# Softmax numerators of three attentions normalised by GpSimd, and a new order of TensorE's work in each block

## The chip, the cores and the metric

One NeuronCore of a Trainium2 (trn2) chip. The metric is the device time of one execution in microseconds (us), the median over runs.

## The reference, cut to what matters

Two transformer layers' worth of blocks over 1024 tokens of width 1024. Three of the stages are attentions with 8 heads of 64 columns: one with a band mask whose entries are log-counts ("attn1"), and two without a mask, in which 8 query heads share 2 key/value heads and the result is multiplied by a gate ("attn2_0", "attn2_1"). Per head, in float32:

```python
scores = q @ k.T * scale            # attn1: + log(count) inside the bands, -1e30 outside
p = softmax(scores, axis=-1)
o = p @ v                           # attn2: o * gate
```

Everything else (feed-forward layers, projections, an mLSTM, a Fourier stage, norms) is outside the change.

## The kernel before, in words

Each engine has its own program, and they meet only through semaphores (`x.at(name, u)` is the value to wait for; `.mark` the signal that is given). All attentions run the same code. The work is cut into blocks u = 0..63 (n = 64), one for 128 queries of one head, and w = u//2 counts pairs of blocks.

TensorE (`attention` of the tensor program, lines 839 to 907), at its step u: `scores(u)` (L858, four 512-column matmuls into one of two PSUM pairs), `turn_over(u-1)` (L868, eight 128x128 transposes of the numerators into the single PSUM pair `p_t`, half 0 then half 1), and the product with V: at odd u the row sums of the two blocks are spread over all partitions (`spread_sum`, L879, a matmul of ones with a diagonal of reciprocals) and then `times_v(w, 0)` with w=(u-3)//2 (L891, eight 256-column matmuls with the high parts); at even u `times_v(w, 1)` with the low parts. `times_v(w, 0)` waits for the low parts of block 2w+1.

ScalarE (lines 1262 to 1309), step u: `half_result` at odd u (copies the lower 64 rows of the V product, L1269; at the end of two heads also the high part of the heads, L1274), `num_high(u-1)` (L1283, the two halves of `p_t` rounded into `th`), `numerators(u)` (L1292, exp with the row sum as accumulator), `diagonal(u-1)` (L1299, identity times the reciprocal).

VectorE (lines 1812 to 1867), step u: `maximum(u)` (attn1: L1824 adds the mask and takes the maximum, L1827 negates it; attn2: L1829), `results` at odd u (L1843 adds the halves of the product, L1847 multiplies by the spread reciprocals; at the end of two heads the gate L1853 and the low part of the heads L1856), `low_parts(u-1)` (L1835, the two halves of `p_t` minus the high parts), the reciprocal of row sum u-1 (L1867).

GpSimd (lines 2130 to 2174) issues the loads of q, k, v, gates, the mask of attn1 (L2227) and, once the last scores are done, the loads of the other half of the mixer's output (`load_mix`, L2174). It computes nothing. SyncE's queue (lines 2234 to 2316) streams the weights through two raw buffers and issues the mLSTM's loads and its last store (L2285).

The order of the work is the order in which each engine's `for u` loop is written; every engine executes its own instructions strictly in that order. After an attention `out_proj` (L600) starts with the k tiles in the order of a list; for attn2 it is tiles 0, 1, 2 of the attention's own heads, then the loaded ones, then tile 3.

Of the kernel before, what the change touches and what calls it, by code (L numbers as in the profile page):

```python
# [13 lines left out]
P = 128  # L14
S = 1024
# [269 lines left out]
def memory(nc, ctx):  # L285
# [105 lines left out]
    def attention_tiles(name, scope, between=None):  # L391
# [10 lines left out]
        a.nu = rings(f"{name}_num", 2, [P, S], F32, scope)  # L402
        a.th = rings(f"{name}_th", 2, [P, ST, 256], F32R, scope)
        a.tl = rings(f"{name}_tl", 2, [P, ST, 256], F32R, scope)
        a.sm = rings(f"{name}_sm", 2, [P, 4], F32, scope)
        a.dg = [t.sqh[1][:, (i + 1) * P:(i + 2) * P] for i in range(3)]
        a.ones = t.sqh[1][:, 0:P]
        a.tm = [t.sqh[0][0:64, i * 256:(i + 1) * 256] for i in range(2)]
# [9 lines left out]
    with ExitStack() as ma:  # L418
        m.mixa = split("mix1a", [P, 4, S], ma)
        with ExitStack() as sc:  # L420
            m.at = attention_tiles("attn1", sc)
            m.at.mask = sb("attn1_mask", [P, 1920], F32, sc)
        mix_tiles(m, "mix1", ma)
# [51 lines left out]
def program_of(nc, ctx, ins, out):  # L475
# [22 lines left out]
    scored, num_turned, spread, pv_done = (signal(n, "PE") for n in ("scored", "num_turned", "spread", "pv_done"))  # L498
# [5 lines left out]
    diag, half_res, mix_hi = (signal(n, "ACT") for n in ("diag", "half_res", "mix_hi"))  # L504
# [6 lines left out]
    mix_lo, ml_dve, conv_dve, four_dve = (signal(n, "DVE") for n in ("mix_lo", "ml_dve", "conv_dve", "four_dve"))  # L511

# [11 lines left out]
    at_const, at_gate, mo_in = signal("at_const_in", "POOL", 16), signal("at_gate_in", "POOL", 16), loaded("mo_in", "POOL", 2)  # L524
# [36 lines left out]
    for n, (kind, _, _, _) in enumerate(plan):  # L561
        if kind == "w":
            split_no[n] = len(split_at)
            split_at.append(n)

# [12 lines left out]
    def tensor_program(e):  # L578
# [260 lines left out]
        def attention(name, mix, kv_of, a, masked):  # L839
# [5 lines left out]
            p_o = ps.take(e, (name, "o"), res_done, name, n // 2 - 1)  # L845
# [16 lines left out]
            def turn_over(u):  # L862
                e.wait_ge(*exped.at(name, u))
                for h in range(2):
                    if u >= 1:
                        e.wait_ge(*num_lo.at(name, u - 1, h))
                    for j in range(4):
                        mm = e.transpose(p_t.half[h][:, j * P:(j + 1) * P], a.nu[u % 2][:, (4 * h + j) * P:(4 * h + j + 1) * P],  # L868
# [3 lines left out]
            def spread_sum(u):  # L872
                w = u // 2
                e.wait_ge(*diag.at(name, u))
                if u == 0:
                    e.wait_ge(*at_const.at(name))
                if w >= 2:
                    e.wait_ge(*res_done.at(name, w - 2))
                mm = e.matmul(p_o.half[w % 2][:, 256 + (u % 2) * P:256 + (u % 2 + 1) * P], a.ones, a.dg[u % 3],  # L879
                              start=True, stop=True)  # L880
                mm.then_inc(*spread.mark(name, u))

            def times_v(w, part):
                hd, i = (2 * w) // ST, (2 * w) % ST
                kv = kv_of(hd)
# [1597 lines left out]
```

## Time and profile before

| | us |
|---|---|
| median of 3 runs (lowest, highest) | 3885.12 (3881.82, 3887.04) |
| the profiled execution | 3889.09 |
| its span in the profile | 3887.3 |
| TensorE busy / VectorE / ScalarE / GpSimd | 3536.8 / 1918.4 / 1351.0 / 149.0 |
| mean granted TensorE clock, share of full speed | 0.951 |

Busy times are sums over the whole span. A row of a timeline says start, duration, engine, line, operation, output<-inputs, shape and count; "x8" with a duration is a merged group, from the first one's start to the last one's end, and the square bracket says how long the engine had been idle and what ended that. A matmul's record is longer than the step to the next one, since they overlap; the distance between starts is the cost.

### The profile page before, as it was taken

Reading aid. Unit: us, or ns where it says so; the run is one execution under the profiler, and the core shown is the slowest. Engines: PE = TensorE matmul, PEld = TensorE weight load, DVE = VectorE, ACT = ScalarE, POOL = GpSimd, SP = SyncE. Lnnn points to the kernel's source line nnn. Section 1 sums busy time; section 2 is a strip of 40 time slices with the busy share of each in tenths; the row PEclk is TensorE's granted clock in tenths of the full one; section 3 lists DMA queues with packets and bytes.
Section 4 is the critical chain, followed back from the end, with each engine's and each line's share of the span. In section 5 each row is a group of like instructions: output and inputs, shape, how many; then the busy total and the mean of one; then the engine's idle time right before and its main releaser. Section 6 shows DMA issues by size and latency. Waiting matters only on the chain.

```text
span 3887.3 us, 41660 instructions
## 1 busy us (share of the span) xinstructions
PE 3536.8 (91%) x17310; PEld 2888.9 (74%) x17310; DVE 1918.4 (49%) x2459; ACT 1351.0 (35%) x1874; POOL 149.0 (4%) x261
## 2 busy tenths in 40 slices
PE   5999999988987698899999998889898988998987
PEld 3888888866975587778888885678887745887875
DVE  6233333366427698353333335622588365137964
ACT  4111111154222388221111113521487064126843
POOL 0000000000100110000000000010100001000000
PEclk8999999999996799999999999999999989999998
DMA  5222221213741453122222221231611103243111
GB/s 194 89 83 71 82 92 66 76 66 98 184 168 39 82 87 61 44 87 71 90 72 78 76 76 38 77 111 60 180 28 33 49 23 102 85 131 98 28 39 44
DMA packets 146619, 316.58 MB, mean 81 GB/s; under 512 B 32616, under 2 KB 96908, under 8 KB 135936
## 3 DMA queue, kind: packets, MB, share of 16 engines
q1 hardware_dynamic: 84880, 216.80, 16.1%
q0 software_dynamic: 61552, 97.12, 10.5%
q8 instruction: 138, 2.26, 0.2%
q14 instruction: 49, 0.40, 0.0%
HBM read 261.79 MB, written 52.09 MB: 81 GB/s over the span
## 4 chain that ended last, share of the span: by engine, by line
PE 79%; DVE 11%; ACT 5%; issue 3%; DMA 1%; POOL 0%; SPq 0%; ACTq 0%; DVEq 0%; POOLq 0%
PE psum L600 56%; PE psum L868 4%; PE psum L891 4%; PE psum L858 4%; PE psum L1015 2%; PE psum L627 2%; PE psum L944 1%; PE psum L698 1%; PE psum L879 1%; DVE h_lo L1495 1%; PE psum L934 1%; ACT attn_th L1283 1%; ACT attn_num L1292 1%; PE psum L792 1%; DVE p_u L1582 0%
## 5 line engine op out<-in xcount | busy, mean ns | idle before, releaser
L600 PE MATMUL psum<-h_hi,w_hi 128*128 128x512 f32 x2112 | 835.0, 395 | 45.0 <-DVE h_lo L1495 26.8
L600 PE MATMUL psum<-h_lo,w_hi 128*128 128x512 f32 x2112 | 826.6, 391 | 0.0
L600 PE MATMUL psum<-h_hi,w_lo 128*128 128x512 f32 x2112 | 826.2, 391 | 0.0
L600 PEld LDWEIGHTS psum<-h_hi,w_hi 128*128 128x128 f32 x2112 | 399.1, 189 | 142.7 <-issue 46.1
L600 PEld LDWEIGHTS psum<-h_lo,w_hi 128*128 128x128 f32 x2112 | 399.4, 189 | 83.1 <-issue 2.9
L600 PEld LDWEIGHTS psum<-h_hi,w_lo 128*128 128x128 f32 x2112 | 399.1, 189 | 83.5
L1051 ACT ACTIVATE w_hi<-w_raw 128x2048 fp32r<-128x2048 f32 (+2 forms) x147 | 249.1, 1695 | 572.1 <-PE psum L600 468.1
L1445 DVE TENSOR_TENSOR w_lo<-w_raw,w_hi 128x2048 fp32r<-128x2048 f32 (+2 forms) x147 | 296.9, 2020 | 262.2 <-ACT w_hi L1051 261.5
L1544 DVE TENSOR_TENSOR gate<-gate,psum 128x1024 f32<-128x1024 f32 x44 | 53.7, 1221 | 608.2 <-PE psum L600 608.2
L600 PE MATMUL psum<-a_hi,w_hi 128*128 128x512 f32 x704 | 274.3, 390 | 3.4 <-DVE a_lo L1546 3.4
L600 PE MATMUL psum<-a_hi,w_lo 128*128 128x512 f32 x704 | 274.1, 389 | 0.0
L600 PE MATMUL psum<-a_lo,w_hi 128*128 128x512 f32 x704 | 274.1, 389 | 0.0
L868 PE MATMUL psum<-mats,attn_num 128*128 128x128 f32 x1536 | 211.7, 282 | 58.1 <-ACT attn_num L1292 56.9
L868 PEld LDWEIGHTS psum<-mats,attn_num 128*128 128x128 f32 x1536 | 177.0, 144 | 112.8 <-ACT attn_num L1292 100.4
L1835 DVE TENSOR_TENSOR attn_tl<-psum,attn_th 128x512 fp32r<-128x512 f32 x384 | 246.4, 681 | 16.3 <-ACT attn_th L1283 15.3
L1560 DVE SCALAR_TENSOR_TENSOR x<-psum,cols,x 128x1024 f32<-128x1024 f32 x80 | 102.7, 1284 | 261.9 <-PE psum L600 261.9
L1283 ACT ACTIVATE attn_th<-psum 128x512 fp32r<-128x512 f32 x384 | 209.1, 594 | 23.6 <-PE psum L868 18.4
L1116 ACT ACTIVATE a_hi<-gate 128x1024 fp32r<-128x1024 f32 x44 | 46.7, 1061 | 478.8 <-DVE gate L1544 478.8
L1829 DVE TENSOR_REDUCE attn_sm<-psum 128x1 f32<-128x1024 f32 x128 | 156.4, 1223 | 39.2 <-PE psum L858 24.8
L858 PE MATMUL psum<-attn_kh,attn_q 128*128 128x512 f32 x384 | 156.0, 406 | 3.9 <-DVE fo_u L1978 2.2
L1111 ACT ACTIVATE gate<-psum 128x1024 f32<-128x1024 f32 x44 | 45.3, 1029 | 318.5 <-PE psum L600 318.5
L858 PE MATMUL psum<-attn_kl,attn_q 128*128 128x512 f32 x384 | 155.7, 406 | 0.0
(332 smaller groups left out, 5703.5 us busy)
## 6 DMA issues: line engine op xcount, KB each, us to landing
w_raw<-in_w_ada SPq DMA_DIRECT2D x52, 1024.0 KB, 5.0
w_raw<-in_w_gu SPq DMA_DIRECT2D x44, 1024.0 KB, 5.4
w_raw<-in_w_in SPq DMA_DIRECT2D x34, 1024.0 KB, 4.8
w_raw<-in_dft SPq DMA_DIRECT2D x16, 1024.0 KB, 5.2
w_raw<-in_w_down SPq DMA_DIRECT2D x24, 512.0 KB, 3.6
w_raw<-in_w_out SPq DMA_DIRECT2D x12, 1024.0 KB, 5.2
w_raw<-in_w_down SPq DMA_DIRECT2D x16, 640.0 KB, 4.3
qk_hi_scratch<-p_out_hi POOLq DMA_DIRECT2D x18, 512.0 KB, 2.9
```

The lines of the kernel that those rows point to most:

```text
L600: mm = e.matmul(p.half[h], a[:, k * width + m * P:k * width + (m + 1) * P], b(k)[:, h * HALF:(h + 1) * HALF], start=(k == order[0] and i = ...
L627: mm = e.matmul(p.full[:, j * 256:(j + 1) * 256], b[:, k, (tt0 + j) * P:(tt0 + j + 1) * P], a[:, k * 256:(k + 1) * 256], start=(k == 0 and ...
L858: mm = e.matmul(p_s[u % 2].half[h], a.q[hd % 2][:, i * P:(i + 1) * P], k_[kv % 2][:, h * HALF:(h + 1) * HALF], start=(j == 0), stop=(j == 1))
L868: mm = e.transpose(p_t.half[h][:, j * P:(j + 1) * P], a.nu[u % 2][:, (4 * h + j) * P:(4 * h + j + 1) * P], ident)
L891: mm = e.matmul(p_o.half[w % 2][:, 0:256], a.v[kv % 2][:, j, :], (a.th, a.tl)[part][w % 2][:, j, :], start=(part == 0 and j == 0), stop=(p ...
L1015: mm = e.matmul(p.half[g][:, 0:256], b[:, g, k, tb * P:(tb + 1) * P], a[:, k * 256:(k + 1) * 256], start=(tb == 0 and k == 0 and i == 0), ...
L1051: e.activation(halves_of(n)[0], raw_of(n), ACT.Identity).then_inc(*w_hi.mark(n))
L1283: e.activation(a.th[w % 2][:, 4 * h:4 * h + 4, c], ps.of[(name, "t")].half[h].rearrange("p (j q) -> p j q", j=4), ACT.Identity).then_inc(* ...
L1445: e.tensor_tensor(lo, raw_of(n), hi.bitcast(F32), ALU.subtract).then_inc(*w_done.mark(n))
L1560: e.scalar_tensor_tensor(out=t.x[:, dd, :], in0=ps.of[("down", n, i, dd)].full, scalar=cols[:, 8 + dd:9 + dd], in1=t.x[:, dd, :], op0=ALU. ...
L1829: e.tensor_reduce(m[:, 1:2], p.full, AX.X, ALU.max, negate=True).then_inc(*maxed.mark(name, u))
L1835: e.tensor_tensor(a.tl[w % 2][:, 4 * h:4 * h + 4, c], ps.of[(name, "t")].half[h].rearrange("p (j q) -> p j q", j=4), a.th[w % 2][:, 4 * h: ...
```

## The change

Six things are changed. (1) GpSimd multiplies each block's numerators in SBUF by the reciprocal of their row sum (`num_scaled`), and TensorE transposes block u only after that; `spread_sum`, `diagonal` and VectorE's multiplication by the spread reciprocals go. (2) TensorE's step u is now scores(u), the V product, turn_over(u-2); the parts of the V product alternate, high parts at even u, low parts at odd u. ScalarE's and VectorE's `num_high` and `low_parts` follow one block later. (3) Results are taken over four blocks (z = 64x512 instead of 64x256), at every fourth step, after the exp of that step on ScalarE and after the low parts on VectorE. (4) The gate's product in attn2 goes from VectorE to GpSimd; the high and low parts of the heads are made at u=22+16pp and u=23+16pp. (5) In attn1 the maximum is taken as a minimum of negated scores, so the negation L1827 goes. (6) The mask is loaded by SyncE's queue into a raw weight buffer, the gates by SyncE's queue too; numerators and sums have three buffers; the keys are loaded in smaller portions, released by scores, not by V products. The load of ones goes.

```diff
-        a.nu = rings(f"{name}_num", 2, [P, S], F32, scope)
+        a.nu = rings(f"{name}_num", 3, [P, S], F32, scope)
-        a.sm = rings(f"{name}_sm", 2, [P, 4], F32, scope)
+        a.sm = rings(f"{name}_sm", 3, [P, 4], F32, scope)
+    t.mix1.at.mask = t.raw[first_out1 % RAW][:, 0:1920]
...
             def turn_over(u):
-                e.wait_ge(*exped.at(name, u))
+                e.wait_ge(*num_scaled.at(name, u))
...
-            def spread_sum(u):
...
             def times_v(w, part):
+                kv, z = kv_of(hd), w // 2
                 if part == 0:
                     e.wait_ge(*num_lo.at(name, 2 * w + 1, 1))
+                    if w % 2 == 0 and z >= 2:
+                        e.wait_ge(*res_done.at(name, z - 2))
...
                 if u < n:
                     scores(u)
-                if 1 <= u <= n:
-                    turn_over(u - 1)
-                if u >= 3 and u % 2 == 1 and u < n + 3:
-                    spread_sum(u - 3)
-                    spread_sum(u - 2)
-                    times_v((u - 3) // 2, 0)
-                if u >= 4 and u % 2 == 0:
-                    times_v((u - 4) // 2, 1)
+                if u >= 4:
+                    times_v((u - 4) // 2, u % 2)
+                if 2 <= u < n + 2:
+                    turn_over(u - 2)
...
+            def half_result(z):
+                e.wait_ge(*pv_done.at(name, 2 * z + 1))
+                if z >= 2:
+                    e.wait_ge(*res_done.at(name, z - 2))
+                e.activation(a.tm[z % 2], ps.of[(name, "o")].half[z % 2][64:128, :], ACT.Identity).then_inc(*half_res.mark(name, z))
+            def heads_high(pp):
+                e.wait_ge(*(res_done.at(name, 4 * pp + 3) if masked else og_gated.at(name, pp)))
+                e.activation(mixa[0][:, pp, :], a.og[:], ACT.Identity).then_inc(*mix_hi.mark(mix, "a", pp))
...
+            for u in range(n + 8):
+                if 2 <= u < n + 2:
+                    num_high(u - 2)
                 if u < n:
                     numerators(u)
-                if 1 <= u <= n:
-                    diagonal(u - 1)
+                if u >= 8 and u % 4 == 0 and u < n + 8:
+                    half_result((u - 8) // 4)
+                if u >= 22 and (u - 22) % 16 == 0:
+                    heads_high((u - 22) // 16)
...
-                    e.wait_ge(*maxed.now())
-                    e.tensor_scalar(m[:, 1:2], m[:, 0:1], -1.0, None, ALU.mult).then_inc(*maxed.mark(name, u))
...
+            def results(z):
+                hh, pp = (z // 2) % 2, z // 4
+                e.wait_ge(*half_res.at(name, z))
+                if z % 4 == 0 and pp:
+                    e.wait_ge(*mix_lo.at(mix, "a", pp - 1))
+                e.tensor_tensor(a.og[64 * hh:64 * hh + 64, (z % 2) * HALF:(z % 2 + 1) * HALF], ps.of[(name, "o")].half[z % 2][0:64, :],
+                                a.tm[z % 2], ALU.add).then_inc(*res_done.mark(name, z))
...
+            for u in range(n + 8):
                 if u < n:
                     maximum(u)
+                if 1 <= u < n + 1:
+                    s = a.sm[(u - 1) % 3]
                     e.wait_ge(*exped.at(name, u - 1))
+                    e.reciprocal(s[:, 3:4], s[:, 2:3]).then_inc(*recip.mark(name, u - 1))
+                if 2 <= u < n + 2:
+                    low_parts(u - 2)
+                if u >= 8 and u % 4 == 0 and u < n + 8:
+                    results((u - 8) // 4)
+                if u >= 23 and (u - 23) % 16 == 0:
+                    heads_low((u - 23) // 16)
...
+        def attention(name, a, n_kv, gated):
             n = A_HEADS * ST
-            e.dma_start(a.ones, ins["mats"][MAT["ones"]]).then_inc(*at_const.mark(name))
             load_kv(name, a, 1)
+            for u in range(n + 8):
+                hd, i = u // ST, u % ST
+                if u < n:
+                    s, m = a.nu[u % 3], a.sm[u % 3]
+                    e.wait_ge(*recip.at(name, u))
+                    e.tensor_scalar(s[:], s[:], m[:, 3:4], None, ALU.mult).then_inc(*num_scaled.mark(name, u))
+                if i == 7 and hd + 2 < A_HEADS:
+                    load_q(name, a, hd + 2)
+                if i in (0, 1) and 1 <= hd < n_kv - 1:
+                    load_k(name, a, hd + 1, i)
+                if i == 3 and 1 <= hd < n_kv - 1:
+                    load_v(name, a, hd + 1)
+                if gated and u >= 20 and (u - 20) % 16 == 0:
+                    pp = (u - 20) // 16
+                    e.wait_ge(*res_done.at(name, 4 * pp + 3))
+                    e.wait_ge(*at_gate.at(name, pp))
+                    e.tensor_tensor(a.og[:], a.og[:], a.g[:], ALU.mult).then_inc(*og_gated.mark(name, pp))
...
+        weights(first_out1 + RAW)
         mlstm()
+        e.wait_ge(*w_done.at(first_out1))
+        e.dma_start(t.mix1.at.mask[:], ins["band"]).then_inc(*at_const.mark("attn1"))
+        e.wait_ge(*maxed.at("attn1", A_HEADS * ST - 1))
         for l in range(2):
             weights(first_block(("dft", l, 0, 0)) + 1 + RAW)
             fourier(l)
+            weights(first_block(("out2", l, 0)) + RAW)
+            attention_gates(l)
```

## Rows read from the trace of the kernel before

**Rows 1.** The page's first part: busy us (share of the span) and instructions

```profile
PE 3536.8 (91%) x17310; PEld 2888.9 (74%) x17310; DVE 1918.4 (49%) x2459; ACT 1351.0 (35%) x1874; POOL 149.0 (4%) x261
```

**Rows 2.** Windows of attn1 and attn2_1: length; busy PE, PEld, DVE, ACT, POOL; clock; DMA

```profile
1316.00:1544.00 228.00, 206.09 (x1417) 179.14 (x1417) 197.16 (x452) 183.38 (x356) 29.59 (x52) 0.95 0.49 81
...
3525.00:3742.00 217.00, 199.08 (x1387) 176.14 (x1388) 190.05 (x323) 178.30 (x355) 13.56 (x25) 0.96 0.17 40
```

**Rows 3.** Timeline of attn2_0, TensorE over one pair of blocks

```profile
2841.36 1.09 PE L868 MATMUL psum<-mats,attn_num 128*128 128x128 f32 x8
...
2842.29 0.61 PE L879 MATMUL psum<-sq 128*128 128x128 f32 x4
...
2842.66 1.19 PE L891 MATMUL psum<-attn_th,attn_v 128*128 128x256 f32 x8
...
2843.69 0.40 PE L858 MATMUL psum<-attn_kh,attn_q 128*128 128x512 f32 x1
...
2844.61 1.04 PE L868 MATMUL psum<-mats,attn_num 128*128 128x128 f32 x8
...
2845.41 1.20 PE L891 MATMUL psum<-attn_tl,attn_v 128*128 128x256 f32 x8
...
2847.48 1.09 PE L868 MATMUL psum<-mats,attn_num 128*128 128x128 f32 x8
```

**Rows 4.** The same timeline, ScalarE and VectorE beside it

```profile
2842.06 1.08 ACT L1283 ACTIVATE attn_th<-psum 128x512 fp32r<-128x512 f32 x2
...
2843.03 1.12 ACT L1292 ACTIVATE attn_num<-psum,attn_sm 128x1024 f32<-128x1024 f32 x1
...
2843.49 1.29 DVE L1835 TENSOR_TENSOR attn_tl<-psum,attn_th 128x512 fp32r<-128x512 f32 x2
```

**Rows 5.** Timeline near the start of attn2_0, where neither engine has a queue

```profile
2798.52 1.09 PE L868 MATMUL psum<-mats,attn_num 128*128 128x128 f32 x8 [0.91 <-ACT attn_num L1292]
2799.21 1.09 ACT L1283 ACTIVATE attn_th<-psum 128x512 fp32r<-128x512 f32 x2 [0.46 <-PE psum L868]
...
2799.84 1.29 DVE L1835 TENSOR_TENSOR attn_tl<-psum,attn_th 128x512 fp32r<-128x512 f32 x2 [0.45 <-ACT attn_th L1283]
```

**Rows 6.** Timeline, one pass of VectorE over 128x1024 from SBUF to SBUF, eight times

```profile
3757.64 4.90 DVE L1988 TENSOR_SCALAR x<-x 128x1024 f32<-128x1024 f32 x8
```

**Rows 7.** Timeline, the start of attn1

```profile
1322.90 0.58 POOL L2227 DMA_DIRECT2D attn_mask<-in_band  x1 [10.71 <-DMA mix_scratch<-ml_o]
...
1328.53 1.23 DVE L1824 CUSTOM_DVE_ANT_0 attn_num<-psum,attn_mask 128x1024 f32<-128x1024 f32 x1 [12.29 <-DMA sq<-in_mats]
...
1331.36 1.97 PE L868 MATMUL psum<-mats,attn_num 128*128 128x128 f32 x8 [10.96 <-ACT attn_num L1292]
```

**Rows 8.** First out_proj matmul behind attn1; first transposes, first out_proj and loaded tile of attn2_1

```profile
1541.52 0.40 PE L600 MATMUL psum<-mix1a_hi,w_hi 128*128 128x512 f32 x1
...
3529.93 1.98 PE psum L868 x8
...
3743.66 0.40 PE L600 MATMUL psum<-mix2a_hi,w_hi 128*128 128x512 f32 x1
...
3751.36 0.80 PE L600 MATMUL psum<-mix21b_hi,w_hi 128*128 128x512 f32 x1 [5.48 <-DVE mix21b_lo L1872]
```

**Rows 9.** The page's DMA part: count, KB each, median us from issue to landing

```profile
mix_t<-mix_scratch POOLq DMA_DIRECT2D x12, 512.0 KB, 4.2
```

**Rows 10.** Timeline of attn1: TensorE behind the second and the third interruption, to the second-next scores

```profile
1445.44 1.09 PE L868 MATMUL psum<-mats,attn_num 128*128 128x128 f32 x8 [2.14 <-ACT attn_num L1292]
...
1450.73 0.40 PE L858 MATMUL psum<-attn_kh,attn_q 128*128 128x512 f32 x1
...
1497.50 1.09 PE L868 MATMUL psum<-mats,attn_num 128*128 128x128 f32 x8 [2.15 <-ACT attn_num L1292]
...
1499.86 0.63 PE L858 MATMUL psum<-attn_kh,attn_q 128*128 128x512 f32 x1
...
1504.14 0.40 PE L858 MATMUL psum<-attn_kh,attn_q 128*128 128x512 f32 x1
```

More of the change, by code:

```diff
@@ L511, in program_of @@
     mix_lo, ml_dve, conv_dve, four_dve = (signal(n, "DVE") for n in ("mix_lo", "ml_dve", "conv_dve", "four_dve"))
+    num_scaled, og_gated = (signal(n, "Pool") for n in ("num_scaled", "og_gated"))
     const_in, x_in = signal("const_in", "SP", 16), loaded("x_in", "SP", 2)
@@ L564, in program_of @@
             split_at.append(n)
+    first_out1 = next(n for n, entry in enumerate(plan) if entry[3] == ("out1", 0))
+    t.mix1.at.mask = t.raw[first_out1 % RAW][:, 0:1920]
     def place_before(n):
@@ L889, in times_v @@
                         e.wait_ge(*v_in[kv % 2].at(name, kv))
+                    if w % 2 == 0 and z >= 2:
+                        e.wait_ge(*res_done.at(name, z - 2))
                 for j in range(ST):
-                    mm = e.matmul(p_o.half[w % 2][:, 0:256], a.v[kv % 2][:, j, :], (a.th, a.tl)[part][w % 2][:, j, :],
-                                  start=(part == 0 and j == 0), stop=(part == 1 and j == ST - 1))
+                    mm = e.matmul(p_o.half[z % 2][:, (w % 2) * 256:(w % 2 + 1) * 256], a.v[kv % 2][:, j, :],
+                                  (a.th, a.tl)[part][w % 2][:, j, :], start=(part == 0 and j == 0),
+                                  stop=(part == 1 and j == ST - 1))
                 if part == 1:
@@ L2214, in block2 @@
             e.wait_ge(*fo_stored.at(l))
[L2215 removed]
+            attention(at_name, m.at, 2, True)
             load_mix(m, mix, at_name, 4)
@@ L2223, in gpsimd_program @@
         fence("attn1")
-        for h in (1, 2):
-            e.wait_ge(*st_stored[h % 2].at("ml", h))
-        e.wait_ge(*ml_stored3.at())
-        e.dma_start(t.mix1.at.mask[:], ins["band"]).then_inc(*at_const.mark("attn1", "mask"))
-        attention("attn1", t.mix1.at, A_HEADS, None)
+        ml_drained(e)
+        attention("attn1", t.mix1.at, A_HEADS, False)
         load_mix(t.mix1, "mix1", "attn1", 0)
@@ L2289, in fourier @@
             e.wait_ge(*passed("PE", f"fourier{l}"))
-            for j in range(2):
+            for j in (0, 1):
                 e.wait_ge(*st_stored[j % 4].at(f"p2b{l}", j))
@@ L2387, in shape_constants @@
     count = (j <= 64).astype(int) + ((j % 4 == 0) & (j <= 256)) + (j % 16 == 0)
-    band = np.where(count > 0, np.log(np.maximum(count, 1)), NEG).astype(f)
+    band = np.where(count > 0, -np.log(np.maximum(count, 1)), -NEG).astype(f)
     sel = np.zeros((36, 8, P), f)
```

145 lines of the change are left out of this document (48 added, 97 removed).

## The prediction

> **What bounds the kernel now.** I read the page first, then the windows of the three attentions, then their timelines. The page says that TensorE is the engine of the whole kernel [rows 1]; the change touches only the attentions, so what counts is what ends last there. The windows show three engines nearly full: in attn1's 228 us TensorE has 206, VectorE 197, ScalarE 183; in attn2_1's 217 us 199, 190 and 178 [rows 2]. Nobody has slack of more than 20%, so an order that makes one engine wait for another costs at once. The timeline gives the beat: two blocks take 6.12 us in attn2 (2841.36 to 2847.48 [rows 3]). TensorE issues in a pair: transposes 2 x 0.80 (2844.61 to 2845.41), V products 2 x 1.04 (2842.66 to 2843.69), scores 2 x 0.92 (2843.69 to 2844.61), the spreading 0.37 (2842.29 to 2842.66, all [rows 3]), and the rest is a short wait for the exp. GpSimd is nearly idle.
>
> The stage lengths, first transposes to first out_proj matmul: attn1 1331.36 to 1541.52 = 210.2 [rows 7, 8], attn2_1 3529.93 to 3743.66 = 213.7 [rows 8]. Attn2_0 has the same pattern and is taken as equal. In them are four interruptions per attention, at each end of two heads, in which TensorE waits for 2 us and more, as 2.14 [rows 10].
>
> **The change, part by part.** *Removed from TensorE:* 0.37 of spreading per pair. If TensorE were alone, a pair would take 2 x (0.92 + 1.04 + 0.80) = 5.52. *Removed elsewhere:* ScalarE loses its diagonals, VectorE the multiplications behind the results and in attn1 the negation. That shortens two engines that already fit beside TensorE, so I count it at nothing; the order below leaves them waiting anyway.
>
> *The new order* is the term that decides. At an even step u, TensorE issues scores(u) and then the V product of the pair whose second block, u-3, was transposed at the very end of step u-1. Before, a whole further step lay between. What this needs is shown where nobody has a queue [rows 5]: transposes start 2798.52, ScalarE's high parts 2799.21, VectorE's low parts 2799.84 to 2801.13, that is 2.61 us, 0.1 less when the transposes themselves had no wait, and 0.05 for the signal: 2.6. TensorE fills only 0.80 + 0.92 = 1.72 of it. So it waits 0.9 in every pair, and its first matmul behind a wait costs 0.1 more (transposes behind a wait take 0.93 to the next group, 2841.36 to 2842.29, against 0.80 [rows 3]). Base pair: 2.60 + 0.10 + 1.04 (V, high) + 0.80 (transposes) + 0.92 (scores) + 1.04 (V, low) = 6.50.
>
> *Results every fourth step.* Count from an odd step's transposes, time 0. Even step: V at 2.6, transposes 3.64, high parts at 4.28, exp at 5.26 (step 0.98 for two halves [rows 4]), which ends at 6.54 with its accumulator; only then half_result, now 64x512, taken as 0.6 like one half of L1283: 7.14. VectorE was done with the low parts at 6.1 and waits; its result runs 7.17 to 7.77 (0.6, like one half of L1835). Behind it are queued the next maximum (1.22, the L1824 row [rows 7]) and reciprocal (0.1): 9.09. Only then low_parts of the odd step: 10.37, while TensorE, which transposed at 6.40, would have had it at 9.0. It waits 1.42 longer, each fourth step, 14 times per attention (steps 8 to 60).
>
> *GpSimd's pass* (128x1024, SBUF to SBUF, scalar per partition) is in no row. Nearest: VectorE's same form takes 4.90/8 = 0.61 [rows 6], ScalarE's and VectorE's passes at full width 1.12 [rows 4] and 1.23 [rows 7]. I bound it by 0.6 below and twice the slowest, 2.5, above, and take 1.2, an engine's ordinary pass. It has room: the reciprocal of block 0 comes at 8.99, and its transposes are due at 11.46, so up to 2.2 it is hidden under the waits above; GpSimd's DMA issues (0.58 [rows 7], at most two behind one pass) fit beside it too. The gate's product there: 1.2 likewise, same ends.
>
> *Ends of heads* (three inside each attention): heads_high (1.06) on ScalarE delays the next high parts by about 0.5, heads_low on VectorE the next maximum by less than its slack: 0.8 each, 2.4 in all. The old interruptions go, since they are in the old lengths.
>
> New length: 31.5 pairs x 6.50 = 204.8, + 14 x 1.42 = 19.9, + last V products 2.6 + 0.1 + 2.08 = 4.8, + 2.4, + 1 for the slow clock at the start = 232.9. Attn1 +22.7; each attn2 +19.2.
>
> *Start.* Attn1's mask now goes behind SyncE's store, which is why GpSimd waited until 1322.90, and needs no buffer of the mLSTM. VectorE still waits for that store, so its first maximum is at about 1323.0, not 1328.53 [rows 7]: -5.5. From first maximum to first transposes 2.83 before, now maximum and exp 2.5, reciprocal and signals 0.3, GpSimd's pass 1.2: 4.0, so +1.2. Net -4.3. Attn2, where TensorE waited for the exp alone: +1.4 each for the reciprocal and the pass. *Tail.* In attn2 load_mix is now queued behind GpSimd's last gate product, which waits for the last result; before it left at the last scores. From TensorE's end: half 0.8, result 1.6, gate 2.9, landing 4.2 after that [rows 9], high part and low part 2.3: 9.5, against 7.7 before (3743.66 to 3751.36 [rows 8]): +1.8 each. In attn1 it is issued behind the last scaling and still covered. The weight block that the mask keeps out is issued at the last maximum, more than 20 us ahead of its use: 0. Gates and keys on other queues: 0, each has over five steps of cover; without it a load of some 4 us would show per head.
>
> Sum: attn1 22.7 - 4.3 = 18.4; attn2 2 x (19.2 + 1.4 + 1.8) = 44.8; together +63. The profiled execution took 3889.09, 4 above the median; the sum is a difference inside it and I put it on the median: 3885.1 + 63 = **3948**.
>
> The page "GPSIMD Engine Reference" of the Trainium skill (section Elementwise — side-by-side cycle accounting) speaks against using that engine: about 2.6 cycles per element for two inputs, 1.03 where the loop is port-bound. By the first rate, an estimate from that page is 2.4 us per pass, over the 2.2 of cover, about 0.2 x 48 = +10 and 3958; by the second it is 1.04 and the sum stands. No row here can tell.
>
> **The rivals.**
> (a) *TensorE is the bound and the new order is harmless:* the place is the V product's wait. If the low parts came back inside 1.72 us of the transposes' start, pairs would take 5.6 and the lengths 187: -23 and -27 twice, with start and tail: 3885 - 75 = 3810. It decides when the mean pair falls below 6.46. For it: TensorE really loses work. Against it: [rows 5], and the order in the code.
> (b) *No stall from the results* (ScalarE's half_result finds a gap): -14 x 1.42 x 3 = -60: 3888. Against: an engine works in order.
> (c) *The clock falls.* Waits of 2.14 us in attn1 left the clock at the 2.4 GHz level in one case, but in the next TensorE went on at 1.2 GHz: a score matmul of 0.63 instead of 0.40 at 1499.86 [rows 10], and from the transposes to the second-next scores it took 1497.50 to 1504.14 = 6.64 instead of 1445.44 to 1450.73 = 5.29 [rows 10], 1.35 more. The new kernel has 14 waits of 2.3 in each attention: all 42 x 1.35 = +57, 4005; a third of them 3967.
> (d) *GpSimd is slower than its cover:* at 3.0 us its pass holds the transposes of even steps 0.8 and 0.5 in four blocks: 1.3 x 48 = +62, 4010.
>
> **How the numbers follow.** Forecast (3920 to 3975) 0.48, (a) 0.12, (b) 0.13, (c) 0.15, (d) 0.12. The range takes in (b), (c) and (d) and leaves (a) out: 3885 to 4012. A measurement can tell about 0.2%, 7.8 us. (b) lies on the border: 0.06 within it, 0.02 faster, 0.05 slower. So faster 0.14, same 0.06, slower 0.80.
>
> **What would show it.** Score starts in the timeline: 14.4 us per four blocks and TensorE waiting for L1835's successor before the V product, 0.9 and 2.3 in turn; VectorE idle before the result until ScalarE's half. TensorE waiting for GpSimd instead is (d); an even beat of 2.8 per block is (a); score matmuls of 0.63 in mid-attention are (c). The forecast is wrong if pairs stay under 6.4 or if the waits are put down to something other than the low parts.

## The result and the profile after

| | us |
|---|---|
| kernel before, median of 4 runs (lowest, highest) | 3883.55 (3881.82, 3887.04) |
| changed kernel, median of 4 runs (lowest, highest) | 4020.82 (4017.36, 4024.97) |
| ratio with its 95% interval | 1.0353 [1.0335, 1.0371] |
| span of the profiled execution, before / after | 3887.3 / 4015.5 |

The change makes the kernel 3.5% slower, 137 us. I had forecast +63 and a range up to 4012; the direction was right, the size too small, and the result lies 9 us above the range.

The page of the changed kernel: the engines' busy time, the shares of the chain that ended last, and five groups (busy us, mean ns of one | idle time before them, and what ended it).

```profile
PE 3548.8 (88%) x16926; PEld 2876.7 (72%) x16926; DVE 1861.8 (46%) x2243; ACT 1279.0 (32%) x1634; POOL 706.9 (18%) x449
...
PE 68%; DVE 13%; POOL 7%; ACT 7%; issue 3%; DMA 2%; SPq 0%; ACTq 0%; DVEq 0%; POOLq 0%
...
L2154 POOL TENSOR_SCALAR attn_num<-attn_num,attn_sm 128x1024 f32<-128x1024 f32 x192 | 545.6, 2846 | 161.6 <-DVE attn_sm L1845 160.7
...
L871 PE MATMUL psum<-mats,attn_num 128*128 128x128 f32 x1536 | 228.6, 296 | 47.9 <-POOL attn_num L2154 45.8
...
L885 PE MATMUL psum<-attn_th,attn_v 128*128 128x256 f32 x768 | 120.9, 302 | 104.6 <-DVE attn_tl L1822 104.6
```

Against [rows 1] every engine but GpSimd issues less: TensorE 384 matmuls fewer, VectorE 216 instructions, ScalarE 240. TensorE is nevertheless busy for 12 us longer: more of its matmuls run at the lower clock (below), and those behind a wait have longer records. GpSimd goes from 4% to 18%, and stands in the chain that ended last with 7%. Its pass takes 2.846 us. TensorE's idle time of the attentions sits mainly at two places: 104.6 us before the first V product, put down to VectorE's low parts, and 45.8 us before the transposes, put down to GpSimd.

Windows of attn1 and attn2_1 (length; busy PE, PEld, DVE, ACT, POOL; clock; DMA), which answer to [rows 2]:

```profile
1324.00:1582.00 258.00, 202.93 (x1270) 170.53 (x1271) 174.47 (x338) 155.12 (x274) 208.26 (x110) 0.95 0.31 63
3635.00:3867.00 232.00, 185.23 (x1152) 157.13 (x1151) 155.11 (x245) 138.10 (x246) 174.24 (x72) 0.94 0.10 26
```

In attn1 no engine is full any more: GpSimd 81%, TensorE 79%, VectorE 68%. Before, TensorE had 90% and VectorE 86% [rows 2]. The stages are bound by latency now (each engine waits in turn for the result of another), and longer. Their starts and ends in the timeline, which answer to [rows 7, 8]:

```profile
1329.45 1.97 PE L871 MATMUL psum<-mats,attn_num 128*128 128x128 f32 x8 [2.43 <-POOL attn_num L2154]
...
1582.28 0.40 PE L603 MATMUL psum<-mix1a_hi,w_hi 128*128 128x512 f32 x1
...
3608.29 1.11 ACT L1285 ACTIVATE attn_num<-psum,attn_sm 128x1024 f32<-128x1024 f32 x1
...
3612.70 1.97 PE L871 MATMUL psum<-mats,attn_num 128*128 128x128 f32 x8 [1.08 <-POOL attn_num L2154]
...
3867.04 0.63 PE L603 MATMUL psum<-mix2a_hi,w_hi 128*128 128x512 f32 x1
...
3877.47 0.79 PE L603 MATMUL psum<-mix21b_hi,w_hi 128*128 128x512 f32 x1 [6.98 <-DVE mix21b_lo L1856]
```

Attn1 from its first transposes to the first out_proj matmul: 1582.28 - 1329.45 = 252.8, before 210.2; attn2_1: 3867.04 - 3612.70 = 254.3, before 213.7. Attn2_0 has 253.9 (2833.53 to 3087.47), before 213.7 (2791.66 to 3005.37), as the forecast had assumed. The three differences, 42.6 + 40.2 + 40.6 = 123.4, are nearly all of the 128.2 by which the spans of the two profiled executions differ.

One stretch of attn1, all engines. It shows both waits and the queue behind them:

```profile
1402.27 0.59 ACT L1260 ACTIVATE sq<-psum 64x512 f32<-64x512 f32 x1
...
1402.89 0.68 DVE L1831 TENSOR_TENSOR attn_o<-psum,sq 64x512 f32<-64x512 f32 x1 [0.94 <-ACT sq L1260]
1403.18 1.09 ACT L1273 ACTIVATE attn_th<-psum 128x512 fp32r<-128x512 f32 x2 [0.32 <-PE psum L871]
...
1403.61 1.23 DVE L1812 CUSTOM_DVE_ANT_0 attn_num<-psum,w_raw 128x1024 f32<-128x1024 f32 x1
...
1404.83 1.27 DVE L1822 TENSOR_TENSOR attn_tl<-psum,attn_th 128x512 fp32r<-128x512 f32 x2
...
1405.03 5.67 POOL L2154 TENSOR_SCALAR attn_num<-attn_num,attn_sm 128x1024 f32<-128x1024 f32 x2 [1.71 <-DVE attn_sm L1845]
...
1406.16 1.23 PE L885 MATMUL psum<-attn_th,attn_v 128*128 128x256 f32 x8 [1.64 <-DVE attn_tl L1822]
...
1407.92 1.09 PE L871 MATMUL psum<-mats,attn_num 128*128 128x128 f32 x8 [0.54 <-POOL attn_num L2154]
```

Read it from the top. ScalarE makes the half result after its exp (1402.27), VectorE waited 0.94 for it and adds (1402.89). Behind that, in VectorE's own order, stands the next maximum (1403.61), and only then the low parts (1404.83). ScalarE's high parts had been there since 1404.27. TensorE, waiting for the low parts, has its V product at 1406.16 after 1.64 us of nothing. That is the forecast's results stall, with its links in the order drawn; the idle time is shorter than the 2.3 drawn. The last two rows are what I had priced at zero: GpSimd's pass started at 1405.03, ends at 1407.88, and the transposes follow it by 0.04.

A stretch in which the clock had fallen, in attn2_0, is the other thing to see:

```profile
2910.38 1.87 PE L871 MATMUL psum<-mats,attn_num 128*128 128x128 f32 x8 [0.55 <-POOL attn_num L2154]
2911.90 0.78 PE L861 MATMUL psum<-attn_kh,attn_q 128*128 128x512 f32 x1
2912.48 0.63 PE L861 MATMUL psum<-attn_kl,attn_q 128*128 128x512 f32 x1
```

The score matmuls last 0.63, where they last 0.40 at the 2.4 GHz level [rows 3]; the granted clock from 2910.38 to 2913 is 0.53. Before the fall TensorE had waited 1.61 and then 0.55. Counted over the three attentions, 90 of the 768 score matmuls last 0.55 us or more, 33 of 768 in the kernel before. Windows of attn2_0 (length; busy PE, PEld, DVE, ACT, POOL; clock; DMA), first the kernel before, then the changed one:

```profile
2791.66:3005.37 213.71, 201.22 (x1400) 178.30 (x1401) 188.28 (x322) 175.72 (x352) 10.09 (x20) 0.97 0.17 38
```

```profile
2833.53:3087.47 253.94, 206.87 (x1268) 175.54 (x1269) 170.94 (x271) 151.64 (x270) 192.14 (x78) 0.93 0.12 25
```

### The profile page after: what moved, and what is told of

Its sections match the earlier page's. It is cut to its first block, busy times and chain, and to the rows that moved or that the text cites. A ratio compares the mean times of both kernels' runs of the same rounds, so it can differ in the third digit from the quotient of the medians.

```text
span 4015.5 us, 40194 instructions
## 1 busy us (share of the span) xinstructions
PE 3548.8 (88%) x16926; PEld 2876.7 (72%) x16926; DVE 1861.8 (46%) x2243; ACT 1279.0 (32%) x1634; POOL 706.9 (18%) x449
## 4 chain that ended last, share of the span: by engine, by line
PE 68%; DVE 13%; POOL 7%; ACT 7%; issue 3%; DMA 2%; SPq 0%; ACTq 0%; DVEq 0%; POOLq 0%
PE psum L603 54%; POOL attn_num L2154 6%; PE psum L1006 2%; PE psum L871 2%; PE psum L630 2%; DVE attn_tl L1822 2%; ACT attn_th L1273 1%; DVE attn_sm L1816 1%; PE psum L885 1%; PE psum L935 1%; PE psum L701 1%; DVE h_lo L1482 1%; PE psum L925 1%; ACT attn_num L1285 1%; PE psum L861 1%
## 5 line engine op out<-in xcount | busy, mean ns | idle before, releaser
L2154 POOL TENSOR_SCALAR attn_num<-attn_num,attn_sm 128x1024 f32<-128x1024 f32 x192 | 545.6, 2846 | 161.6 <-DVE attn_sm L1845 160.7
L871 PE MATMUL psum<-mats,attn_num 128*128 128x128 f32 x1536 | 228.6, 296 | 47.9 <-POOL attn_num L2154 45.8
L885 PE MATMUL psum<-attn_th,attn_v 128*128 128x256 f32 x768 | 120.9, 302 | 104.6 <-DVE attn_tl L1822 104.6
L885 PEld LDWEIGHTS psum<-attn_th,attn_v 128*128 128x128 f32 x768 | 100.5, 195 | 145.1 <-DVE attn_tl L1822 145.1
L861 PE MATMUL psum<-attn_kh,attn_q 128*128 128x512 f32 x384 | 180.1, 469 | 22.4 <-ACT attn_num L1285 12.6
```

What stands on the lines that cost most here:

```text
L861: mm = e.matmul(p_s[u % 2].half[h], a.q[hd % 2][:, i * P:(i + 1) * P], k_[kv % 2][:, h * HALF:(h + 1) * HALF], start=(j == 0), stop=(j == 1))
L885: mm = e.matmul(p_o.half[z % 2][:, (w % 2) * 256:(w % 2 + 1) * 256], a.v[kv % 2][:, j, :], (a.th, a.tl)[part][w % 2][:, j, :], start=(part ...
L2154: e.tensor_scalar(s[:], s[:], m[:, 3:4], None, ALU.mult).then_inc(*num_scaled.mark(name, u))
```

## The experiments

All are edits of the changed kernel unless said otherwise. Where no interval is given it is one time, beside one or more runs of the kernel before on the same chip; those runs lie up to 11 us apart (3878.72 to 3890.14), so differences of some 10 us between such times are weak.

### How long GpSimd's pass is, and what the order costs without it

```diff
-                    e.tensor_scalar(s[:], s[:], m[:, 3:4], None, ALU.mult)
+                    e.tensor_scalar(s[:, 0:8], s[:, 0:8], m[:, 3:4], None, ALU.mult)
```

> GpSimd multiplies only 8 of the 1024 columns of each block, so that its pass costs almost nothing and every wait and the order stay; the other columns stay unscaled. Theory A (two causes: my forecast's waits of the order, and on top of them a GpSimd pass of 2.85 us where I had 1.2): what is left is my forecast without the pass in start and tail, about 3943 us. Rival B (the GpSimd pass alone is the cause, the new order costs nothing): TensorE-bound pairs, about 3810 us. Rival C (a pass of GpSimd is not what holds the transposes, its semaphores or the clock are): stays near 4020.

**Measured: 3946.39**, the kernel before 3885.36 beside it, so +61.0. TensorE's idle groups:

```profile
L871 PE MATMUL psum<-mats,attn_num 128*128 128x128 f32 x1536 | 210.8, 283 | 0.4
...
L885 PE MATMUL psum<-attn_th,attn_v 128*128 128x256 f32 x768 | 118.1, 297 | 123.5 <-DVE attn_tl L1822 123.5
```

The wait for GpSimd is gone from the transposes (0.4 us), the wait before the V product stays and even grows. So 61 of the 137 us are there without the pass, and about 75 come from its length. The 61 belong to the new order with all else that was changed beside it; the edits of order below show that the order is what costs. A stretch of attn2_1, without the end of a head and at the full clock:

```profile
3605.23 0.48 PE L861 MATMUL psum<-attn_kh,attn_q 128*128 128x512 f32 x1
...
3608.27 1.22 PE L885 MATMUL psum<-attn_th,attn_v 128*128 128x256 f32 x8 [1.87 <-DVE attn_tl L1822]
...
3610.12 0.48 PE L861 MATMUL psum<-attn_kh,attn_q 128*128 128x512 f32 x1
...
3614.69 1.22 PE L885 MATMUL psum<-attn_th,attn_v 128*128 128x256 f32 x8 [0.64 <-DVE attn_tl L1822]
...
3619.29 0.48 PE L861 MATMUL psum<-attn_kh,attn_q 128*128 128x512 f32 x1
```

The waits of 1.87 and 0.64 come in turn. Four blocks take 3619.29 - 3605.23 = 14.06 by the score starts; I had forecast 14.4. That is the shortest that occurs: over the 42 groups of four blocks with a result in them the mean is 14.67, since the ends of heads and stretches at the lower clock come on top.

With half the columns (`s[:, 0:512]` in the same line; the others stay unscaled here too):

> GpSimd multiplies 512 of 1024 columns, so that its pass is about 1.45 us, near the 1.2 of the forecast; the other columns stay unscaled. Theory A: below the 2.2 us of cover, so about 3948 us, no more than 6 above the run with 8 columns. Rival B: a pass of 1.45 fits beside TensorE too: about 3815 us. Rival C: near 4020.

**Measured: 3960.63.** The pass takes 1.563 us. And the full product, written with another instruction:

```diff
-                    e.tensor_scalar(s[:], s[:], m[:, 3:4], None, ALU.mult)
+                    e.tensor_tensor(s[:], s[:], m[:, 3:4].to_broadcast([P, S]), ALU.mult)
```

> Full pass, but as a tensor_tensor product with the reciprocal column broadcast along the row, since the gate's product of that form took 2.36 us and the tensor_scalar pass 2.85. Theory A: a pass of 2.4 is 0.2 over the cover of 2.2 on every other block, about 3960 to 3985 us, much under 4020. If the pass takes 2.85 us in this form too, about 4020.

**Measured: 3956.34**, with the whole computation done. The four GpSimd groups, of the kernels with 8 columns, 512 columns, the other instruction, and (last row) the deeper kernel with the first instruction:

```profile
L2154 POOL TENSOR_SCALAR attn_num<-attn_num,attn_sm 128x8 f32<-128x8 f32 x192 | 58.6, 305 | 573.0 <-DVE attn_sm L1845 573.0
```

```profile
L2154 POOL TENSOR_SCALAR attn_num<-attn_num,attn_sm 128x512 f32<-128x512 f32 x192 | 300.1, 1563 | 341.0 <-DVE attn_sm L1845 340.8
```

```profile
L2154 POOL TENSOR_TENSOR attn_num<-attn_num,attn_sm 128x1024 f32<-128x1024 f32 x192 | 363.4, 1893 | 282.1 <-DVE attn_sm L1845 281.9
```

```profile
L2155 POOL TENSOR_SCALAR attn_num<-attn_num,attn_sm 128x1024 f32<-128x1024 f32 x192 | 546.0, 2859 | 7.3 <-DVE attn_sm L1846 5.8
```

So passes of 0.31, 1.56, 1.89 and 2.85 us give 3946, 3961, 3956 and 4021; the three stage lengths together are 697.5, 702.8, 705.3 and 761.1. From 0.3 up to 1.9 the pass costs 10 to 14 us in all, hardly more than two runs of one kernel can differ, of which the three starts of the attentions, where it has no cover, are 3 x 1.6 = 5; from 1.9 to 2.85 it costs 64 more. There is a cover, and its end lies between those two values, where the forecast had put it (2.2).

### V product and transposes in the other order

```diff
-                if u >= 4:
-                    times_v((u - 4) // 2, u % 2)
                 if 2 <= u < n + 2:
                     turn_over(u - 2)
+                if u >= 4:
+                    times_v((u - 4) // 2, u % 2)
```

> Full GpSimd pass, but TensorE transposes before the V product in each step, the rest as changed. The V product then no longer waits for the low parts, but the scaled numerators are due 1.04 us earlier. Theory A with the chain scores 1.13, maximum 1.23, reciprocal 0.25, pass 2.85 between the scores of step u-1 and the transposes of step u: a block of about 4.5 us instead of 4.04, so slower than the changed kernel, about 4100 us. Rival (the V product's wait is the larger cost): faster than 4020, about 3960.

**Measured: 4050.13**, 29 us slower than the changed kernel: the sign that my theory named, at well under half the size. The waits of attn2_0, 2870 to 3060 (total us, times, longest):

```profile
ACT attn_th L1273 <- PE psum L871: 74.0, 44, 3.0
...
PE psum L871 <- POOL attn_num L2154: 45.4, 30, 2.7
```

The low parts no longer hold TensorE: the wait before the V product has been bought off with a longer one before the transposes. The chain is scores, maximum, exp, reciprocal, pass, transposes, and with transposes first it has lost the V product's 1.04 as cover. With a pass of this length either order stalls. What the order is worth can only be seen with the pass out of the way, so the next two use 8 columns.

### Results at the head of the step, then the order, with a short pass

```diff
             for u in range(n + 8):
+                if u >= 8 and u % 4 == 0 and u < n + 8:
+                    half_result((u - 8) // 4)
                 if 2 <= u < n + 2:
...
                     numerators(u)
-                if u >= 8 and u % 4 == 0 and u < n + 8:
-                    half_result((u - 8) // 4)
...
-                if 2 <= u < n + 2:
-                    low_parts(u - 2)
                 if u >= 8 and u % 4 == 0 and u < n + 8:
                     results((u - 8) // 4)
+                if 2 <= u < n + 2:
+                    low_parts(u - 2)
```

> Again GpSimd multiplies only 8 of the 1024 columns (the rest stays unscaled), TensorE's order as changed, but ScalarE takes half_result at the head of its step, before the high parts and the exp, and VectorE takes results before its low parts. Theory A: the longer wait of each fourth step goes, 14 x 1.42 x 3 = 60 us off the 3946 of the run with 8 columns: about 3886 us, and the wait of about 0.9 before the V product stays in every pair. Rival (the two waits are one and the same, or results are not what delays the low parts): within 15 us of 3946.

**Measured: 3870.76**, 75.6 below the same kernel without this edit, or 72.5 when each is taken against the kernel before on its own chip (forecast of the stall's price: 60). A pair now is the same nearly everywhere; only at the ends of heads is it up to 0.4 longer:

```profile
2869.23 0.48 PE L861 MATMUL psum<-attn_kh,attn_q 128*128 128x512 f32 x1
...
2871.05 1.22 PE L885 MATMUL psum<-attn_th,attn_v 128*128 128x256 f32 x8 [0.64 <-DVE attn_tl L1822]
...
2872.90 0.48 PE L861 MATMUL psum<-attn_kh,attn_q 128*128 128x512 f32 x1
...
2875.65 0.48 PE L861 MATMUL psum<-attn_kh,attn_q 128*128 128x512 f32 x1
```

2875.65 - 2869.23 = 6.42, made of 3.67 and 2.75, against a forecast base pair of 6.50. The 0.64 (idle time; the start is 1.05 after the last score matmul's) is the wait that the order of the code makes. Attn2_0 and the sums over the three stages, first without the early results, then with them:

```profile
2809.03:3042.32 233.29, 191.96 (x1269) 168.81 (x1268) 170.97 (x271) 151.13 (x270) 32.48 (x78) 0.96 0.13 29
...
sum 697.52, PE 573.69 PEld 504.63 DVE 513.25 ACT 455.87 POOL 109.91; mean PE 191.23 PEld 168.21 DVE 171.08 ACT 151.96 POOL 36.64
```

```profile
2781.17:2988.68 207.51, 183.92 (x1269) 161.80 (x1268) 169.48 (x271) 149.06 (x270) 32.61 (x78) 0.99 0.15 32
...
sum 622.86, PE 551.93 PEld 485.51 DVE 509.33 ACT 449.60 POOL 110.27; mean PE 183.98 PEld 161.84 DVE 169.78 ACT 149.87 POOL 36.76
```

The stages are 74.7 us shorter. TensorE, which issues the same matmuls in the same order, is idle for 52.9 us less and busy for 21.8 less, and its granted clock goes from 0.96 to 0.99. So the stall itself cost some 53 us, 42 x 1.22 = 51 by the score starts (four blocks in 14.06, now in 2 x 6.42), and the rest goes with the clock that had fallen behind the waits. Then the transposes come first as well:

> As the run before it (8 columns scaled, early results), and TensorE transposes before the V product. Theory A: no wait is left but TensorE's own work, 2.76 us a block, lengths of about 183 us: about 3800 us. Rival (VectorE with 2.65 us a block and ScalarE keep TensorE from it): about 3850 us.

**Measured: 3802.97**, another 67.8 off. A window of its attn2_0:

```profile
2790.00:2840.00 50.00, 48.91 (x351) 43.70 (x350) 46.70 (x76) 41.55 (x76) 9.73 (x23) 1.00 0.13 33
```

TensorE is busy for 98% of it at a clock of 1.00, and most blocks take 2.76, which is half of the 5.52 I had worked out for TensorE alone; with one longer block in four the mean is 2.88. Behind the first 12 us of each stage no score matmul lasts 0.55 us or more. The kernel is 79 us faster than the one before. That takes together the spreading matmuls, the waits for the exp and the old interruptions at the ends of heads (see the last experiment); no run here separates them. The same early results with the full product, V first and the faster instruction:

> Complete: the changed kernel with two edits, GpSimd's pass as tensor_tensor (1.9 us) and the early half_result and results; TensorE's order stays V first. Theory A: a pass of 1.9 us stays under the cover, and the pair is 6.4 us with the short wait before the V product alone: 3871 (the run with 8 columns) and up to 10 for the pass in start, tail and the blocks where a DMA issue stands behind it: 3871 to 3885 us, so about the kernel before. Rival: the pass and the results add up, near 3956.

**Measured: 3884.07** beside 3883.74: as fast as the kernel before, within the noise. Removing the results stall and a third of the pass pays back the whole loss, and no more; V still waits (22 us of idle time in each stage).

### A complete kernel with one block more between the steps

It has the faster instruction, transposes before V, both a block later, four buffers for the numerators in attn1, and the results at the head of steps 9, 13, ...:

```diff
-        a.nu = rings(f"{name}_num", 3, [P, S], F32, scope)
+        a.nb = 4 if name == "attn1" else 3
+        a.nu = rings(f"{name}_num", a.nb, [P, S], F32, scope)
-        a.sm = rings(f"{name}_sm", 3, [P, 4], F32, scope)
+        a.sm = rings(f"{name}_sm", 4, [P, 4], F32, scope)
...
-                if u >= 4:
-                    times_v((u - 4) // 2, u % 2)
-                if 2 <= u < n + 2:
-                    turn_over(u - 2)
+                if 3 <= u < n + 3:
+                    turn_over(u - 3)
+                if u >= 5:
+                    times_v((u - 5) // 2, (u - 5) % 2)
...
+                if u >= 9 and u % 4 == 1:
+                    half_result((u - 9) // 4)
+                if 3 <= u < n + 3:
+                    num_high(u - 3)
```

(The old lines of ScalarE's loop go; VectorE's loop likewise, with the results ahead of `low_parts(u - 3)`.)

> Complete. GpSimd's pass as tensor_tensor with the broadcast reciprocal (1.89 us in the run of that form); transposes before the V product and one block later (turn_over(u-3)), with four numerator buffers in attn1; half_result and results at the head of their steps, at u = 9, 13, ... Theory A: GpSimd has two blocks for its pass, so it is off the path, the V product has a full step for the low parts, and TensorE's 2.76 to 2.85 us a block remain: 3805 to 3830 us, faster than both kernels. Rival (GpSimd's 1.89 plus DMA issues, or VectorE, set the block at about 3.1): near 3885.

**Measured: 3812.69** (3807.93 to 3816.59), ratio to the kernel before **0.9811 [0.9795, 0.9828]**. It is 1.9% faster than the kernel before, and beats both kernels. TensorE in attn2_0:

```profile
2852.13 0.40 PE L862 MATMUL psum<-attn_kh,attn_q 128*128 128x512 f32 x1
...
2853.05 1.03 PE L872 MATMUL psum<-mats,attn_num 128*128 128x128 f32 x8
2853.85 1.20 PE L886 MATMUL psum<-attn_th,attn_v 128*128 128x256 f32 x8
2854.89 0.40 PE L862 MATMUL psum<-attn_kh,attn_q 128*128 128x512 f32 x1
```

Scores 0.92, transposes 0.80, V product 1.04: 2.76, with nothing between them in this stretch; a whole stage takes 185 to 188 us. Three runs change one thing each in this kernel. First, V goes ahead of the transposes again:

> Complete: the deep version (3812.7) with one edit, TensorE takes the V product ahead of the transposes in each step. Theory A: the wait before the V product comes back, 0.9 us in each of 32 pairs of three attentions: +86, about 3895 us. Rival (the block later hides it): 3815.

**Measured: 3876.25**, +63.6. The order of the two is worth that much here too. The block more lies between a block's scores and its transposes; between its transposes and its V product the distance is the old one, as both moved, so the wait for the low parts comes back whole (71.2 us in all, against 70.6 in the run with early results alone). Second, the `tensor_scalar` instruction comes back:

> Complete: the deep version with one edit, GpSimd's pass as tensor_scalar again (2.85 us). Theory A: with two blocks of cover the latency no longer counts, but GpSimd's own time per block does: in attn1 2.85 and 0.5 of DMA issues on average against a block of about 2.85 us, +32; in each attn2 2.85 and 0.2 to 0.3, +16: about 3875 us. Rival (the latency of the pass counts still): above 3920.

**Measured: 3862.69**, +50.0. GpSimd waited here for the reciprocals for only 5.8 us in all (the last of the four rows above): 2.86 of pass is more than the 2.76 of a block, and its loads and the gate's product come on top, so GpSimd has become the engine that sets the beat. A greater distance can't hide that; this follows from the rows, and no run here tries one. The third moves the first three loads of the mixer's tiles ahead of the last gate product (`early` issues them):

```diff
+                if u == n and early is not None:
+                    early()
```

> Complete: the deep version with one edit, in both attn2 GpSimd issues the first three loads of load_mix right behind its last scaling pass, not behind the gate's last product. Theory A: the loads are then down before ScalarE asks for them, so the first loaded tile is ready about 2 to 3 us earlier, twice: 4 to 6 us under 3812.7, a ratio of about 0.980 to the kernel before. Rival (something else holds the first tile): same as the deep version, 0.9811.

**Measured: 3816.11** (3811.39 to 3820.19), ratio 0.9820 [0.9807, 0.9834] against 0.9811 [0.9795, 0.9828]: no gain, a miss. The chain that ended last says where it went. First the kernel without the edit, then with it:

```profile
3679.16 3.76 DMA mix_t<-mix_scratch
...
3685.31 84.89 PE psum L604 x366
```

```profile
3677.69 3.83 DMA mix_t<-mix_scratch
...
3683.91 86.09 PE psum L604 x366
```

The last loaded tile comes 1.5 us sooner and the matmuls start 1.4 sooner, but the same 366 matmuls take 1.2 us longer. In the first kernel they start with 0.50, 0.39 and 0.39 us, the 2.4 GHz level, and 8 or so at the lower level follow; in the second the first 13 or so all last 0.63 and more. In attn2_0 it is 1.6 sooner and 1.0 longer. So in these two traces most of the shorter wait was given back by the clock. And the loads had not been all that the stage waited for: with them early, ScalarE's high part of the first loaded tile is released by VectorE's low part of the gated tile.

```profile
3674.98 2.95 ACT L1302 ACTIVATE mix21b_hi<-mix_t 128x1024 fp32r<-128x1024 f32 x3 [1.34 <-DVE mix2a_lo L1837]
```

### The ends of heads, in the kernel before

The forecast said that the old interruptions go with the change. This run takes only that: in the kernel before, ScalarE's high part of the heads goes from the head of its step to the end, and VectorE's low part to the step after, so that no block waits behind them.

```diff
-                if hd % 2 == 1 and i + 2 >= ST:
-                    pp = hd // 2
-                    e.wait_ge(*res_done.at(name, "heads", pp))
-                    e.activation(mixa[0][:, pp, :], a.og[:], ACT.Identity).then_inc(*mix_hi.mark(mix, "a", pp))
...
+                if u >= 19 and (u - 19) % 16 == 0:
+                    heads_high((u - 19) // 16)
```

> The kernel before with one edit: the high and the low part of finished heads are made later (ScalarE at the end of step 19+16pp, VectorE in step 20+16pp) so that no engine waits for them in the middle of a step. The interruptions at the ends of heads cost 1.7 us in attn1 and about 4.8 in attn2, three times each: 34 us if all of it goes, 3850; if the gate's product on VectorE stays on the path about 8 us of that stay, 3858. Rival: they only shift the stall by a step: 3883.

**Measured: 3861.61** (3858.67 to 3864.94), ratio 0.9942 [0.9927, 0.9956]. Some 21 us (3882.23 beside it) were to be had in the old kernel by that alone; I had expected 3850 or 3858. The changed kernel defers these parts too, so its losses are net of a gain of this kind.

## Why the forecast was right in direction and wrong in size

**The step that failed** is the one on GpSimd's pass: "I bound it by 0.6 below and twice the slowest, 2.5, above, and take 1.2, an engine's ordinary pass." It takes 2.846 us (2.835 to 2.873 over 192 of them), more than twice the value taken and above the upper bound. The bound was drawn from rows of other engines, and nothing in those rows speaks for GpSimd. A sign that I had named showed it: of TensorE's 150 us of idle time at the two places, 45.8 were put down to GpSimd and not to the low parts. The rest of the step held: "up to 2.2 it is hidden" agrees with the runs, in which 1.89 cost almost nothing and 2.85 cost 64 more. Rival (d), at 3.0 us, was worked out as 1.3 per four blocks; 64.5 / 48 is 1.34. On top of the forecast it gives its 4010, against 4021 measured. That nearness is in part luck: four blocks at the full clock grew from 14.06 to 15.22 only (in attn2_1 from 3628.37 to 3643.59), by 1.16, and lower clock and ends of heads made up the rest, which (d) had not counted. I gave it 0.12, and my range ended almost at it, with no room for the order's and the clock's own spread above it.

The Trainium skill's page "GPSIMD Engine Reference" (section Elementwise — side-by-side cycle accounting) gives 2.6 cycles per element for two inputs, which I had costed at 2.4 us and 3958. For an instruction with two full operands the measurement agrees with that estimate (the gate's product, 2.361 us). The pass has one full operand, and at 2.846 us it takes longer than even the two-input estimate; the estimate of 1.04 us from the 1.03 cycles of the same section is too low by a factor of 2.7.

**The order's own price came out right, in part by luck.** With the pass nearly gone the kernel is 61 us slower than before, where I expected 58 (3943). Inside it the two terms were right in kind and a little large: the pair of 6.50 measured 6.42, the results stall of 1.42 measured 1.22. By these two alone a stage would be 31.5 x 0.08 + 14 x 0.20 = 5.3 us shorter than the 232.9 of the forecast, and yet the stages took 233.8, 233.3 and 230.5. What fills the gap is the lower clock, for which the forecast had only 1 us at the start of a stage; it is why removing the results stall gave 75.6 and not some 53. The V wait gave 67.8. That the two sum to more than 61 is the gain rival (a) had named: without either wait the kernel is at 3803, 79 below the one before (3882.23 beside it), and (a) had said 3810, 75 below. Rival (a) as such, "the new order is harmless", is refuted; its price for TensorE alone is right to 4 us. Rival (b), no stall from the results, is refuted by the same pair of runs.

**Starts and tails** came out as drawn once the right durations stand in them. Attn2's start: from the first exp to the first transposes 4.41 (3608.29 to 3612.70), before 1.26 (3528.67 to 3529.93); that is +3.15, forecast +1.4, and of the missing 1.75 the pass is 1.65, being 2.85 and not 1.2. Tail: 10.43 (3867.04 to 3877.47) for a forecast of 9.5; the gate's product, 2.37 us and not 1.2, would add 1.17, and the other parts were together 0.24 shorter. Attn1's start gained 1.9 and not 4.3: its first maximum came at 1323.66 (forecast 1323.0), then the same 1.65 again.

**The clock, rival (c),** was not the main cause but has a part. It had 42 slow stretches at 1.35 us, 57 us, or 19 for a third of them. Slow score matmuls went from 33 to 90 of 768. The three stages held 35 us at the 1.2 GHz level before and 90 after by the clock in the trace (granted clock 0.98, 0.97, 0.97 before, 0.96, 0.93, 0.94 after). From one score matmul to the next it is 0.43 us at the lower level and 0.23 at the upper (2912.48 and 2870.01 are in such stretches), about half, so an estimate is that at most 27 of the 137 us are the clock's. In the run with 8 columns it was 57 us (78 slow score matmuls), so at most 11 of them belong to the order's 61. The early results brought it down to 10 us (30), with 21.8 us less of busy time. No run holds the waits and changes only the clock, so this share is worked out, not shown.

**Sum.** Order 61 + pass about 75 make up the 137, each with its share of the clock. The parts overlap where both hold TensorE, and the split between them is by this sequence of edits.

**Contention** I had not priced: GpSimd reads and writes 1024 columns of SBUF beside a busy VectorE. In the changed kernel none is seen: the passes differ by 0.04 us over the whole kernel, and VectorE's low parts have a mean of 685 ns beside them against 683 in the kernel with the 8-column pass. In the deeper kernels it is seen, at VectorE's low part of the heads, a subtraction with both inputs in SBUF, which takes 1.22 us alone. First the kernel with `tensor_scalar` at the longer distance, then the one with the faster instruction:

```profile
1399.11 1.22 DVE L1837 TENSOR_TENSOR mix1a_lo<-attn_o,mix1a_hi 128x1024 fp32r<-128x1024 f32 x1
...
1399.33 3.70 POOL L2155 TENSOR_SCALAR attn_num<-attn_num,attn_sm 128x1024 f32<-128x1024 f32 x1
```

```profile
2828.95 1.97 DVE L1837 TENSOR_TENSOR mix2a_lo<-attn_o,mix2a_hi 128x1024 fp32r<-128x1024 f32 x1
```

The first pass started 0.22 us into the subtraction and took 3.70 and not 2.85. It happened three times in that run. The second subtraction started 1.02 us into a pass that took 1.91, and took 1.97 itself, in all six cases inside attn2 (1.80 in the three of attn1). These are some 0.9 us for GpSimd or 0.6 to 0.8 for VectorE, at the end of two heads only, and no part of the 137; of the +50.0 of the `tensor_scalar` run they can be up to 3.

## What to carry to other kernels

Before moving work to an engine that does nothing in the kernel, get one duration of that very instruction on that engine; a row of another engine bounds nothing. Where engines run in order, price a reordering by the distance from the producer's issue to the consumer's need: here the new order cost 61 us even with the pass nearly gone, although every engine but GpSimd had less to do, and the same work with transposes first, results at the head of the step, a block more of distance and the faster form of the pass is 1.9% faster than the kernel before. A shorter wait after which TensorE is at the lower clock may be paid back in the matmuls that follow, so look at the run of matmuls behind it too.

## What the runs showed of the hardware that I had not expected

- On GpSimd a product with one scalar per partition (`tensor_scalar`) took 0.305, 1.563 and 2.846 us for 8, 512 and 1024 columns: about 2.5 ns for each further column. The same product as `tensor_tensor` with the column broadcast took 1.893 us, a third less. With two full operands (the gate) it took 2.361.
- Beside a VectorE subtraction with both inputs in SBUF either engine could be held: a pass that started 0.22 us after it took 3.70 us and not 2.85 (three times), and the subtraction took 1.80 or 1.97 us and not 1.22 where it started 1.2 or 1.0 us into a broadcast pass. In the changed kernel it overlapped passes by up to 1.19 us with nothing lost.
- A wait of 1.4 us less in front of 366 matmuls returned 0.2 us, and in attn2_0 one of 1.6 us returned 0.6, since more of the matmuls behind it ran at the lower clock.
- Taking 53 us of waits out of TensorE's way made the same matmuls 21.8 us shorter in busy time, as the granted clock rose from 0.96 or 0.97 to 0.99.
